# Turns, sines and cosines of the state-space tiles moved from the second attention layer to the first, and a new place for the memory sums behind the bias stores

## The chip, the cores and the metric

The kernel runs on one NeuronCore of a Trainium2 chip. The metric is device microseconds for one execution; a time is the median of several runs.

The core has five instruction streams: TensorE (PE, with its weight loads shown as PEld), VectorE (DVE), ScalarE (ACT), GpSimd (POOL) and SyncE (SP, which here only issues transfers). They run by themselves and are tied together by semaphores: an instruction waits for a count, another raises it. ACT and POOL issue transfers too; such an issue stands in the rows as ACTq or POOL, and the transfer itself runs on 16 DMA engines.

## What is computed

Two transformer blocks over 256 tokens of width 2048, all in fp32. The first has two layers of 16 heads of three kinds, the second has one state-space mixer, one differential attention and a feed-forward part. Cut to what matters here:

```python
for l in range(2):                                   # first block
    h = rms_norm(x, norm_g[l]);  z = h @ w_in[l]     # 6 neighbourhood, 6 dilated, 4 memory heads
    o_na = neighbourhood_attention(..., na_rpb[l])   # needs a bias table for each head
    o_dl = dilated_attention(rope(q), rope(k), v)
    mk, mv = split(rms_norm(mem, mem_norm_g) @ w_mem_kv[l])     # needs the sum of squares of mem
    o_m  = memory_attention(m_q, mk, mv)
    x = x + concat(o_na * silu(..), o_dl * silu(..), o_m * silu(..)) @ w_out[l]
x = rms_norm(x, final_g)

dt   = exp(log_step);  mag = exp(lr * dt)            # second block, state-space mixer
ab_r = mag * cos(li * dt);  ab_i = mag * sin(li * dt)
# s[t] = ab * s[t-1] + B u[t];  y[t] = Re(C s[t]) + d * u[t],  64 groups x 64 states
```

The state-space scan is not run step by step. For each of 32 tiles (two groups of 64 states, 128 partitions) the kernel makes a table from the parameters alone, and stores it to `tab_d` in HBM, where the second block reads it. A table holds the columns e (2 x 128), the lags k (128), the cosines and sines of the angle at 64 chunk starts (64 + 64) and the columns f (2 x 128). Nothing in a table depends on x.

## The kernel before, in words

**Matmuls in two parts.** Each weight chunk (128 x 1024, 512 KB) is loaded by SP into a ring of four `w_raw` buffers, ScalarE makes its high part `w_hi` (`split_hi`, L752), VectorE the rest `w_lo` (`split_lo`, L1404), and TensorE multiplies high by high, high by low and low by high (L2221 to L2223, or L2233 and L2234 where two products are joined). `w_hi` of a chunk may be written once TensorE has used the chunk four before.

**Head periods.** In the first block the unit of work is a head period of eight chunks (four jobs of two). `head_period` is written once for each engine. While the projections of head g stream through TensorE, the attention of head g-1 and the gating of head g-2 run in between: scores (L2258), `softmax_max`, `softmax_exp`, `softmax_scale` on VectorE (reciprocal L1491, two multiplies L1494), the transposition of the probabilities (L2267), and their product with v (L2276). Each layer has 16 head periods, in the order dilated, neighbourhood, memory, with `evac` and `evac_rope` (L1452 to L1461) on VectorE to empty the PSUM banks.

**The memory norm in layer 0.** In the eight periods 4 to 11 ScalarE squares `mem` (`mem_blocks`, L822, L825) and POOL adds the squares up in `msq_sum` (L618, 16 additions of 128 x 256). ScalarE's next square of the loop waits for POOL's addition before.

**Bias tables.** `na_bias` on POOL makes one neighbourhood head's bias of 128 x 512: a transfer into `na_pad_d` (L558), four into `na_raw` (L567), an addition of the mask (L571), and a store to `na_bias_d` (L573), whose landing it waits for before it returns (L574, `na_stored`). POOL makes six of these ahead of the memory sums and six after them.

**The tables in layer 1.** Each of the 16 periods of layer 1 makes two tiles, an even one (between the third and the fourth job's chunks) and an odd one (at the period's end). POOL multiplies up the powers (L597, L598, L601, into `xt`), TensorE transposes e and makes k (L2299, L2301), and then `tile` on ScalarE (L786 to L809) stores f (L789, 128 KB), copies e into `tab_out` (L792), prepares the next tile (L773, L775), computes the sine and cosine of `turns` (Sin table load L800, L801, L803, L805), waits for VectorE's lags and stores e, k, cosines and sines together (L809, 256 KB). VectorE makes `turns` in `tile_turns` (five instructions of 128 x 64, L1520 to L1529) and k in `tile_lags` (four of 32 rows, L1538), the latter not before the store of the tile before has landed (`tab_stored`). Sin and the Tanh of the gate sit in different tables of ScalarE, hence the table loads.

Order on every engine is program order as written; there is no scheduler.

## Time and profile before

| | |
|---|---|
| median of three runs | 2418.33 us (2418.19 to 2419.38) |
| the profiled execution | 2421.73 us |
| its span in the trace | 2420.0 us |
| TensorE busy | 2400.7 us |
| VectorE busy | 1714.1 us |
| ScalarE busy | 1218.7 us |
| GpSimd busy | 526.8 us |
| granted TensorE clock, mean | 0.999 |

The profiled execution took 3.4 us more than the median, and 1.7 us of it lie outside the span. The page gives busy times of the whole; which wait matters is read from the idle time in front of single TensorE instructions, which stands in brackets behind a row with the engine whose work ended it.

### The profile page before, as it was taken

What the parts mean: (1) busy time and instruction counts of PE and PEld (TensorE: products, weight loads), DVE (VectorE), ACT (ScalarE), POOL (GpSimd) and SP (SyncE); (2) the same over time, 40 slices, a digit from 0 to 9 for tenths busy, and PEclk for the clock granted to TensorE, in tenths of its full rate; (3) what the DMA queues carried; (4) which work ended last, traced back from release to release, by engine and by line L of the source; (5) the groups of instructions that cost most, each with busy time, mean ns of one, the idle gap of its engine ahead of it and who ended that gap; (6) DMA issues with size and microseconds to landing.
All of it is one profiled execution on the core that took longest, in us unless ns stands there. A gap on an engine that the chain in (4) does not pass through costs nothing.

```text
span 2420.0 us, 45086 instructions
## 1 busy us (share of the span) xinstructions
PE 2400.7 (99%) x15288; PEld 2170.0 (90%) x15288; DVE 1714.1 (71%) x2644; ACT 1218.7 (50%) x1834; POOL 526.8 (22%) x1002
## 2 busy tenths in 40 slices
PE   9999999999999999999999999999999999999999
PEld 7878888998999999999999999998888888888888
DVE  8877776668888887678888876666555555555556
ACT  6444454455666665556665444444444444444442
POOL 2210032246767773210021221111000000000000
PEclk9999999999999999999999999999999999999999
DMA  7756576666666665565567777756777777777774
GB/s 253 238 177 199 187 227 202 197 195 197 192 205 210 198 197 183 184 203 188 161 196 248 257 224 232 232 193 186 199 191 191 191 191 190 190 190 192 190 190 151
DMA packets 257244, 485.07 MB, mean 200 GB/s; under 512 B 23704, under 2 KB 171876, under 8 KB 256880
## 3 DMA queue, kind: packets, MB, share of 16 engines
q1 hardware_dynamic: 216208, 415.66, 56.5%
q10 hardware_dynamic: 29632, 35.30, 4.6%
q0 software_dynamic: 11296, 32.68, 4.5%
q8 instruction: 67, 1.10, 0.2%
q14 instruction: 41, 0.34, 0.1%
HBM read 455.20 MB, written 31.08 MB: 201 GB/s over the span
## 4 chain that ended last, share of the span: by engine, by line
PE 82%; DVE 7%; DMA 4%; issue 3%; ACT 2%; POOL 1%; ACTq 0%; DVEq 0%; SPq 0%; POOLq 0%
PE z_ps L2233 12%; PE z_ps L2221 9%; PE z_ps L2222 9%; PE z_ps L2223 9%; PE z_ps L2649 7%; PE z_ps L2650 7%; PE z_ps L2655 7%; PE z_ps L2234 6%; DVE w_lo L1404 3%; DMA arena<-na_pad_d 1%; ACT w_hi L752 1%; DMA na_pad_d<-na_one_d 1%; DMA na_bias_d<-arena 1%; PE o_ps L2276 1%; PE s_ps L2258 1%
## 5 line engine op out<-in xcount | busy, mean ns | idle before, releaser
L1404 DVE TENSOR_TENSOR w_lo<-w_raw,w_hi 128x1024 fp32r<-128x1024 f32 x518 | 641.1, 1267 | 215.9 <-ACT w_hi L752 213.9
L752 ACT ACTIVATE w_hi<-w_raw 128x1024 fp32r<-128x1024 f32 x518 | 528.5, 1050 | 229.6 <-PE z_ps L2234 115.7
L2089 DVE TENSOR_TENSOR w_lo<-w_raw,w_hi 128x1024 fp32r<-128x1024 f32 x262 | 320.8, 1226 | 300.5 <-ACT w_hi L1244 300.5
L2233 PE MATMUL z_ps<-x_both,w_hi 128*128 128x512 f32 x1432 | 513.3, 401 | 0.7 <-DVE w_lo L1397 0.5
L1244 ACT ACTIVATE w_hi<-w_raw 128x1024 fp32r<-128x1024 f32 x262 | 277.9, 1061 | 415.3 <-PE z_ps L2655 267.8
L2234 PE MATMUL z_ps<-x_both,w_lo 128*128 128x256 f32 x1432 | 401.2, 280 | 0.0
L2221 PE MATMUL z_ps<-x_both,w_hi 128*128 128x256 f32 x1376 | 397.8, 289 | 1.1 <-DVEq L1941 0.8
L2223 PE MATMUL z_ps<-x_both,w_lo 128*128 128x256 f32 x1376 | 389.3, 283 | 0.0
L2222 PE MATMUL z_ps<-x_both,w_hi 128*128 128x256 f32 x1376 | 389.2, 283 | 0.0
L2233 PEld LDWEIGHTS z_ps<-x_both,w_hi 128*128 128x128 f32 x1432 | 269.6, 188 | 63.6 <-DVE w_lo L1397 0.8
L2649 PE MATMUL z_ps<-w_hi,x_both 128*128 128x512 f32 x704 | 275.0, 391 | 0.0
L2650 PE MATMUL z_ps<-w_hi,x_both 128*128 128x512 f32 x704 | 274.1, 389 | 0.0
L2234 PEld LDWEIGHTS z_ps<-x_both,w_lo 128*128 128x128 f32 x1432 | 270.9, 189 | 0.5
L2221 PEld LDWEIGHTS z_ps<-x_both,w_hi 128*128 128x128 f32 x1376 | 263.7, 192 | 8.1 <-issue 4.8
L2222 PEld LDWEIGHTS z_ps<-x_both,w_hi 128*128 128x128 f32 x1376 | 263.8, 192 | 0.5
L2223 PEld LDWEIGHTS z_ps<-x_both,w_lo 128*128 128x128 f32 x1376 | 263.6, 192 | 0.0
L2221 PE MATMUL z_ps<-y_hi,w_hi 128*128 128x256 f32 x736 | 210.2, 286 | 0.0
L2222 PE MATMUL z_ps<-y_lo,w_hi 128*128 128x256 f32 x736 | 208.2, 283 | 0.0
L2223 PE MATMUL z_ps<-y_hi,w_lo 128*128 128x256 f32 x736 | 208.2, 283 | 0.0
L2655 PE MATMUL z_ps<-w_lo,x_both 128*128 128x512 f32 x704 | 188.2, 389 | 0.0
L2655 PEld LDWEIGHTS z_ps<-w_lo,x_both 128*128 128x128 f32 x704 | 132.1, 188 | 27.5
L2650 PEld LDWEIGHTS z_ps<-w_hi,x_both 128*128 128x128 f32 x704 | 132.2, 188 | 27.2
(474 smaller groups left out, 4186.9 us busy)
## 6 DMA issues: line engine op xcount, KB each, us to landing
w_raw<-in_w SPq DMA_DIRECT2D x624, 512.0 KB, 4.3
w_raw<-in_w SPq DMA_DIRECT2D x160, 256.0 KB, 3.3
w_raw<-in_w SPq DMA_DIRECT2D x80, 384.0 KB, 4.9
w_raw<-in_w SPq DMA_DIRECT2D x80, 128.0 KB, 3.0
tab_d<-arena ACTq DMA_DIRECT2D x32, 256.0 KB, 3.0
res<-tab_d POOLq DMA_DIRECT2D x16, 384.0 KB, 5.6
arena<-tab_d POOLq DMA_DIRECT2D x16, 384.0 KB, 6.1
tab_d<-arena ACTq DMA_DIRECT2D x32, 128.0 KB, 2.8
```

The costliest lines, as they stand in the source:

```text
L752: act.activation(w_hi[:, n % RING, :], w_raw[:, n % RING, :], ACT.Copy).then_inc(w_hi_ready, 1)
L1244: act.activation(w_hi[:, k % RING, :], w_raw[:, k % RING, :], ACT.Copy).then_inc(w_hi_ready, 1)
L1404: dve.tensor_tensor(w_lo[:, n % RING, :], w_raw[:, n % RING, :], w_hi[:, n % RING, :].bitcast(F32), ALU.subtract).then_inc(w_lo_ready, 1)
L2089: dve.tensor_tensor(w_lo[:, k % RING, :], w_raw[:, k % RING, :], w_hi[:, k % RING, :].bitcast(F32), ALU.subtract).then_inc(w_lo_ready, 1)
L2221: pe.matmul(z, wh, hi[:, kt, :], start=(first and i == 0), stop=False)
L2222: pe.matmul(z, wh, lo[:, kt, :], start=False, stop=False)
L2223: m = pe.matmul(z, wl, hi[:, kt, :], start=False, stop=(last and i == len(kts) - 1))
L2233: pe.matmul(z[:], wh, both[:, :, kt, :], start=(first and kt == kts[0]), stop=False)
L2234: m = pe.matmul(z[:, 0, :], wl, both[:, 0, kt, :], start=False, stop=(last and kt == kts[-1]))
L2649: pe.matmul(z[t], x_hi[:, kt, r], hi_w[:, :, i * P:(i + 1) * P], start=(kt == 0), stop=False)
L2650: pe.matmul(z[t], x_lo[:, kt, r], hi_w[:, :, i * P:(i + 1) * P], start=False, stop=False)
L2655: m = pe.matmul(z[t], x_hi[:, kt, t * P:(t + 1) * P], lo_w[:, :, i * P:(i + 1) * P], start=False, stop=(kt == KT - 1))
```

## The change

1. **Turns and trigonometry.** `tile_turns` (VectorE) and the four ScalarE activations of each tile are gone from layer 1. POOL makes the turns of four tiles at once (`four_turns(j)`, eight instructions of 128 x 256), and ScalarE their sines and cosines (`four_trigs(j)`, four activations of 128 x 256 and a store of 256 KB to `tab_d`), once in each of the eight layer-0 periods 4 to 11. The first group's turns stand behind the first two memory sums, the others ahead of theirs. `t_vec` is loaded by SP at the start, not by ScalarE in period 12.
2. **Bias and memory sums on POOL.** The wait for `na_stored` goes from the end of `na_bias` to just before `na_raw` is written again, and is made once more after the twelfth. POOL starts its bias transfers before it waits for the first squares of x.
3. **The stores of a tile.** f is stored as before; e is stored alone from a double buffer (L840 of the new file, 128 KB) right after its copy, with no wait for the lags; the lags have one buffer `k_out` and a store of 64 KB of their own, issued by ScalarE only when it comes to the next tile, ahead of that tile's f. `tile_lags` waits for this store (`k_stored`) where it waited for `tab_stored`.

```diff
@@ na_bias, POOL
                 pool.wait_ge(pad_stored, 16 * lh + 16)
+                reach(pool, na_stored, 16 * lh)
...
                 pool.dma_start(na_bias_d[lh], flat).then_inc(na_stored, 16)
-                pool.wait_ge(na_stored, (lh + 1) * 16)
@@ POOL, layer 0
-            with pool.Fori(0, KT) as n:
-                pool.wait_ge(msq_ready, n + 1)
-                pool.wait_ge(msq_summed, n + 1)
-                pool.tensor_tensor(msq_sum[:], msq_sum[:], msq[:], ALU.add).then_inc(msq_summed, 1)
+            def four_turns(j):
+                reach(pool, trig_ready, j)
+                f, f_hi, f_lo = (ssm_f[:, i, 4 * j:4 * j + 4].unsqueeze(2).to_broadcast([P, 4, NC]) for i in range(3))
+                pool.tensor_tensor(turn_k, times_in, f, ALU.mult)
+                pool.tensor_tensor(turn_d, times_in, f_hi, ALU.mult)
+                pool.tensor_tensor(turns, times_in, f_lo, ALU.mult).then_inc(turn_step, 1)
+                pool.wait_ge(turn_step, 5 * j + 1)
+                pool.tensor_scalar(turn_k, turn_k, ROUND, None, ALU.add).then_inc(turn_step, 1)
...
+                pool.tensor_scalar(turns, turns, 0.5, -0.5, ALU.min, ALU.max).then_inc(turns_ready, 1)
+            for j in range(KT // 2):
+                if j == 0:
+                    sum_mem(2 * j)
+                    sum_mem(2 * j + 1)
+                    four_turns(j)
+                else:
+                    four_turns(j)
+                    sum_mem(2 * j)
+                    sum_mem(2 * j + 1)
             pool.wait_ge(sums_ready, 1)
+            pool.wait_ge(trig_stored, 16 * ST // 4)
@@ tile, ScalarE, layer 1
                 act.wait_ge(ek_done, st + 1)
+                if not (isinstance(st, int) and st == 0):
+                    lags_store(st - 1)
...
-                reach(act, tab_stored, 16 * st)
-                act.activation(tab_out[:, 0:2 * P], tile_bank(bank_of(st, e))[0], ACT.Copy).then_inc(e_ready, 1)
+                reach(act, tab_stored, 16 * (st - 1))
+                act.activation(e_out[e], tile_bank(bank_of(st, e))[0], ACT.Copy).then_inc(e_ready, 1)
...
-                act.wait_ge(turns_ready, st + 1)
-                act.activation(tab_out[:, 3 * P + NC:4 * P], turns, ACT.Sin, scale=TURN)
...
-                act.wait_ge(m_ready, st + 1)
-                act.dma_start(tab_d[st][:, 0:4 * P], tab_out).then_inc(tab_stored, 16)
+                act.wait_ge(e_ready, st + 1)
+                act.dma_start(tab_d[st][:, 0:2 * P], e_out[e]).then_inc(tab_stored, 16)
+            def lags_store(st):
+                act.wait_ge(m_ready, st + 1)
+                act.dma_start(tab_d[st][:, 2 * P:3 * P], k_out).then_inc(k_stored, 16)
+            def four_trigs(j):
+                act.wait_ge(turns_ready, j + 1)
...
+                act.activation(trig_out[:, :, 1, :], turns, ACT.Sin, scale=TURN)
...
+                act.dma_start(tab_d[bass.ds(4 * j, 4), :, 3 * P:4 * P].rearrange("s p x -> p s x"),
+                              sq_sum.rearrange("p a (s x) -> p (a s) x", x=P)).then_inc(trig_stored, 16)
@@ tile_lags, VectorE, layer 1
-                reach(dve, tab_stored, 16 * st)
+                reach(dve, k_stored, 16 * st)
@@ head_period, VectorE (at two places)
-                if l == 1:
-                    tile_turns(2 * h)
@@ head_period, ScalarE, at the end of a memory-norm period
+                if mem is not None:
+                    four_trigs(mem)
```

On POOL, at the end of the first six bias tables, the order was (L573 is the bias store, L618 the memory sum, in a loop, L620 the clearing of `sq_sum` behind the sixteenth):

```order
L573 DMA na_bias_d<-arena 128x512 [waits na_added]
L615 UNCONDITIONAL_BRANCH [waits na_stored]
L615 ISA
L618 TENSOR_TENSOR arena<-arena 128x256 [waits msq_summed,msq_ready]
L615 REGISTER_ALU
L615 COMPARE_AND_BRANCH
L620 MEMSET arena 128x512 [waits sums_ready]
```

and is now (L578 the bias store, L621 the memory sum, L629 to L641 the turns of four tiles):

```order
L578 DMA na_bias_d<-arena 128x512 [waits na_added]
L621 TENSOR_TENSOR arena<-arena 128x256 [waits msq_ready,msq_summed,consts_landed,param_sums]
L621 TENSOR_TENSOR arena<-arena 128x256 [waits msq_summed,msq_ready]
L629 TENSOR_TENSOR arena<-arena,ssm_f 128x256
L630 TENSOR_TENSOR arena<-arena,ssm_f 128x256
L631 TENSOR_TENSOR arena<-arena,ssm_f 128x256
L633 TENSOR_SCALAR arena<-arena 128x256 [waits turn_step]
L635 TENSOR_SCALAR arena<-arena 128x256 [waits turn_step]
L637 TENSOR_TENSOR arena<-arena 128x256 [waits turn_step]
L639 TENSOR_TENSOR arena<-arena 128x256 [waits turn_step]
L641 TENSOR_SCALAR arena<-arena 128x256 [waits turn_step]
L629 TENSOR_TENSOR arena<-arena,ssm_f 128x256 [waits trig_ready]
```

The sums no longer wait for `na_stored`, and eight instructions of turns stand between each pair of sums and the next.

On ScalarE, at an even tile of a neighbourhood period of layer 1, the order was (L830 loads the next head's bias, L789 stores f, L792 copies e, L800 to L805 are the sine and cosine, L809 is the common store):

```order
L830 ISA [waits biased]
L830 DMA arena<-na_bias_d 128x512
L788 ISA
L789 ISA [waits ek_done]
L789 DMA tab_d<-arena 128x2x128
L404 REGISTER_ALU
L792 ACTIVATE arena<-z_ps 128x256 [waits tab_stored]
...
L800 ACT_TABLE_LOAD
L800 ACTIVATE arena<-arena 128x64 [waits turns_ready]
...
L809 REGISTER_ALU [waits m_ready,e_ready,tab_ready]
L809 DMA tab_d<-arena 128x512
```

and is now (L883 the bias, L847 the lags of the tile before, L831 f, L834 the copy of e, L840 its store):

```order
L883 ISA [waits biased]
L883 DMA arena<-na_bias_d 128x512
L828 ISA
L847 ISA [waits m_ready,ek_done]
L847 DMA tab_d<-arena 128x128
L831 ISA
L831 DMA tab_d<-arena 128x2x128
L407 REGISTER_ALU
L834 ACTIVATE arena<-z_ps 128x256 [waits tab_stored]
...
L840 REGISTER_ALU [waits e_ready]
L840 DMA tab_d<-arena 128x256
```

The store of the lags of the tile before stands behind the bias load, ahead of the f store, and the wait for VectorE's lags behind the tile is gone.

On VectorE, between the third job's weights and the scaling of the probabilities, the lags now wait for that store (L1458 is `split_lo`, L1575 the lags, L1545 and L1548 the scaling):

```order
L1458 TENSOR_TENSOR w_lo<-w_raw,w_hi 128x1024 [waits w_hi_ready]
L1571 ISA
L407 REGISTER_ALU [waits e_ready]
L1575 ISA [waits k_stored]
L1575 SCALAR_TENSOR_TENSOR arena<-ident,ssm_em,z_ps 32x128
...
L1575 SCALAR_TENSOR_TENSOR arena<-ident,ssm_em,z_ps 32x32
L1545 RECIPROCAL cols<-cols 128x2 [waits exp_done]
L1548 TENSOR_SCALAR arena<-arena,cols 128x256 [waits factor_ready]
```

The order itself is the one of before; the count that the four lag instructions wait for is raised by another, later store, and the probabilities' scaling stands behind them.

## Rows read from the trace of the kernel before

**Rows 1.** The page: span, and busy time of each engine.

```profile
span 2420.0 us, 45086 instructions
...
PE 2400.7 (99%) x15288; PEld 2170.0 (90%) x15288; DVE 1714.1 (71%) x2644; ACT 1218.7 (50%) x1834; POOL 526.8 (22%) x1002
```

**Rows 2.** Windows: stretch, its length, busy PE, PEld, DVE, ACT, POOL; clock, DMA.

```profile
100.00:200.00 100.00, 94.21 (x530) 81.89 (x528) 82.47 (x166) 47.40 (x74) 15.11 (x20) 0.98 0.62 196
500.00:700.00 200.00, 194.65 (x1357) 180.10 (x1356) 168.25 (x318) 122.47 (x240) 131.58 (x286) 1.00 0.62 196
700.00:950.00 250.00, 250.00 (x1755) 233.54 (x1754) 204.10 (x379) 158.64 (x321) 172.00 (x371) 1.00 0.63 205
```

**Rows 3.** Timeline, PE, layer 0: start, duration, instruction, [idle before <- releaser].

```profile
136.22 1.13 PE L2276 MATMUL o_ps<-arena 128*128 128x256 f32 x4 [2.86 <-ACT arena L857]
...
158.36 1.07 PE L2267 MATMUL p_ps<-ident,arena 128*128 128x128 f32 x4 [2.93 <-DVE arena L1494]
...
159.86 0.63 PE L2233 MATMUL z_ps<-x_both,w_hi 128*128 128x512 f32 x1
...
162.53 0.39 PE L2233 MATMUL z_ps<-x_both,w_hi 128*128 128x512 f32 x1
```

**Rows 4.** Timeline, ACT: two rows of layer 0, and a table load of layer 1.

```profile
133.37 0.42 ACT L825 ACTIVATE arena<-arena 128x256 f32<-128x256 f32 x1 [7.72 <-POOL arena L618]
...
137.47 2.01 ACT L752 ACTIVATE w_hi<-w_raw 128x1024 fp32r<-128x1024 f32 x2
...
775.61 1.28 ACT L800 ACT_TABLE_LOAD   x1
```

**Rows 5.** POOL: two timeline rows, one of the waits, one of the lines.

```profile
20.03 2.57 POOL L545 TENSOR_TENSOR arena<-arena 128x1024 f32<-128x1024 f32 x1 [17.46 <-ACT arena L922]
...
132.61 0.73 POOL L618 TENSOR_TENSOR arena<-arena 128x256 f32<-128x256 f32 x1 [2.08 <-DMA na_bias_d<-arena]
...
POOL na_pad_d L558 <- DMA na_bias_d<-arena: 32.1, 10, 4.4
...
L618 POOL TENSOR_TENSOR arena<-arena 128x256 f32<-128x256 f32 x16 | 14.4, 903 | 162.4 <-ACT arena L825 160.3 <-DMA na_bias_d<-arena 2.1
```

**Rows 6.** Timeline, DVE and POOL: two of layer 0, two beside each other later.

```profile
142.58 2.35 DVE L1404 TENSOR_TENSOR w_lo<-w_raw,w_hi 128x1024 fp32r<-128x1024 f32 x2
...
157.41 0.89 DVE L1494 TENSOR_SCALAR arena<-arena,cols 128x256 f32<-128x256 f32 x2
...
520.39 2.59 POOL L601 TENSOR_TENSOR arena<-arena 128x64 f32<-128x64 f32 x2
...
520.32 2.49 DVE L1404 TENSOR_TENSOR w_lo<-w_raw,w_hi 128x1024 fp32r<-128x1024 f32 x2
```

**Rows 7.** Timeline, an even tile in layer 1: ACT and its queue, DVE, PE.

```profile
772.95 1.06 ACT L752 ACTIVATE w_hi<-w_raw 128x1024 fp32r<-128x1024 f32 x1 [1.26 <-PE z_ps L2223]
773.72 0.39 ACTq L789 DMA_DIRECT2D tab_d<-arena  x1
...
775.18 1.22 DVE L1538 SCALAR_TENSOR_TENSOR arena<-ident,ssm_em,z_ps 32x128 f32<-32x128 f32 x4
...
776.63 0.62 DVE L1494 TENSOR_SCALAR arena<-arena,cols 128x256 f32<-128x256 f32 x2
...
778.41 0.60 PE L2267 MATMUL p_ps<-ident,arena 128*128 128x128 f32 x4
```

**Rows 8.** Timeline, PE, layer 1: three rows with idle time.

```profile
547.23 0.44 PE L2256 MATMUL v_ps<-ident,arena 128*128 128x128 f32 x2 [1.40 <-DVE arena L1436]
...
562.36 0.63 PE L2267 MATMUL p_ps<-ident,arena 128*128 128x128 f32 x4 [1.07 <-DVE arena L1494]
...
591.02 0.41 PE L2299 MATMUL z_ps<-ident,arena 128*128 128x128 f32 x2 [0.80 <-POOL arena L597]
```

**Rows 9.** The f store: landings of L789 from 700 to 950, and one in 773:779.

```profile
DMA to landing us min/median/max: 1.8/2.5/4.6
...
tab_d<-arena ACTq DMA_DIRECT2D x1, 128.0 KB, 4.6
```

92 lines of the change are left out of this document (45 added, 47 removed).

## The prediction

> **What bounds the kernel now.** I read the page first. TensorE is busy 2400.7 of 2420.0 us [rows 1], so the most that any change off TensorE can give back is its idle time and the time it spends at a lower clock. VectorE, ScalarE and GpSimd have room on average, so an instruction less on them counts only where TensorE stands and waits for it. The windows come second, since they say where TensorE's idle time lies: 5.79 us in 100 to 200, 5.35 us in 500 to 700, none in 700 to 950 [rows 2]. The change touches both halves of that: the memory norm lies in the first stretch, the state-space tiles from 520 on. Last, TensorE's timeline gives the waits one by one.
>
> In layer 0 there are two. At 136.22 TensorE waits 2.86 us for ScalarE's L857, at 158.36 it waits 2.93 us for VectorE's L1494 [rows 3]. Both come from one place. ScalarE stood 7.72 us at 133.37 for POOL's memory sum [rows 4], and POOL came to its first sum at 132.61, when its sixth bias store had landed [rows 5]. So everything after ran late: w_hi of the next period at 137.47 [rows 4], w_lo at 142.58, L1494 at 157.41 [rows 6]. Behind the second wait the granted clock fell: the same matmul takes 0.63 us at 159.86 and 0.39 us at 162.53 [rows 3]. That is the lower of the two levels (1.2 and 2.4 GHz) for some 3.4 us; a pair of L2233 and L2234 then takes 0.64 instead of 0.35 us, so about 1.8 us is lost. Together about 7.9 us, counting 0.3 of small idles.
>
> In layer 1 three waits matter: 1.40 us at 547.23 for L1436, 1.07 at 562.36 for L1494, 0.80 at 591.02 [rows 8]. For the last the trace names POOL's L597; VectorE's emptying of the bank by L1454 ended after it, and it is the same bank, so I put it down to VectorE. Several smaller ones make up the 5.35 us.
>
> **The bias tables and the memory sums.** POOL starts its bias chain behind L545, which waited 17.46 us for ScalarE and ran from 20.03 for 2.57 us [rows 5]. The transfers for the bias pad and its copy now go ahead of that wait, which brings the chain forward by about 8 us (my reading of the chain: three transfers, of which two are now done by 20, and 2.57 of L545 beside the third). Each of the five further tables waited for the store before it: 32.1 us in 10 such waits, 3.2 each [rows 5]. That wait now comes behind the pad transfer, which takes longer than the store, so 5 x 3.2 = 16.0 go; the last store's 2.08 us go too. 132.61 - 8 - 16.0 - 2.1 gives 106.5, while ScalarE first needs a sum at 133.37 - 7.72 = 125.65. POOL is 19 us ahead, and the 7.72 us wait goes even if half of this estimate is wrong.
>
> **The turns and the trigonometry in layer 0.** Behind ScalarE's two squares of period 4 there now stand, for the first group, eight POOL instructions of 128 x 256. The nearest row is the memory sum of that shape: 0.73 us alone, 903 ns on average over 16 [rows 5]; so 8 x 0.73 to 8 x 0.90, 5.8 to 7.2 us, plus some 0.1 us for each hop between dependent ones. They start at about 127.4 and end between 133.7 and 136. ScalarE's part is four activations of that shape, 0.42 us for a square [rows 4], 1.7 us, with one gap 2.3 us. The Sin table is in place for the first group; the seven others add one load each, 1.28 us [rows 4], and the Tanh load on the way back. So ScalarE starts w_hi of the next period at 136 to 138, where it started at 137.47 [rows 4]. The change takes 7.7 us out of this place and puts 5 to 8 us back into the same place. TensorE's first wait (2.86 us for L857) goes, since L857 stands ahead of the trigonometry. VectorE's parameter work, which ran from 138.1 to 142.5 between two chunks, now runs while ScalarE waits, and w_lo starts when w_hi has come, 137 to 139 instead of 142.58. L1494 ends 15.7 us after that start (157.41 + 0.89 - 142.58 [rows 6]), so at 153 to 155. TensorE was done with what stands ahead at 158.36 - 2.93 = 155.4, and without the first wait at 152.5. Left of the second wait: 0.7 to 3.6 us; I take 2.1, with 0.4 for a chance of the lower clock. Layer 0 gives back 7.9 - 2.5 = 5.4 us (2 to 7.5). In the other seven periods ScalarE has about 1.7 us in hand at each of eight chunks, where it waits for TensorE, and VectorE 2.0 us ahead of L1494; 3 to 4.3 us of added ScalarE work at the period's end is inside that, and I put it at nothing. If the cover is gone, it costs what exceeds it, at most 1 us in each.
>
> Moving the t_vec load to SP at the start costs nothing: the constants had landed at about 16 us, and their reader, ScalarE, was busy until 18.
>
> **The tables in layer 1.** Gone are 32 x 5 VectorE instructions and, on ScalarE, 32 x 4 activations, the Sin loads (1.28 us each, one to a tile pair or so [rows 4]) and the Tanh loads. VectorE's chain behind the norm of x gets shorter by about 3.9 us, which takes the waits at 547.23 and most of 562.36. With the small ones of the stretch I count 6.5 us gone. Beyond that nothing can be gained: from 700 on TensorE has no idle time to lose [rows 2].
>
> Added is a wait. tile_lags used to wait for the common store of the tile before, long landed. Now it waits for k_stored, which ScalarE issues only when it reaches this tile, just ahead of its f store. At the even tile of a neighbourhood period f was issued at 773.72, lags ran from 775.18, L1494 behind them ended at 776.63 + 0.62 = 777.25, and TensorE's L2267 started at 778.41 without a wait [rows 7]. So the store had 1.46 us until the lags could start and there were 1.16 us of slack behind: it may take 2.6 us from issue to landing at no cost. What stands behind the waiting instruction on VectorE is L1545 and L1548 (the scaling, L1494 before), and TensorE's L2267 waits for them; next the bank of the fourth job.
>
> No row shows a store of 64 KB. The nearest is the f store from the same queue and the same place, with twice the bytes: 1.8, 2.5 and 4.6 us to landing (min, median, max), and 4.6 in the very period above [rows 9]. At the fourteen even tiles from 4 on, it was 2.5 to 2.9 six times, 3.5 once, and 3.8 to 4.6 seven times. The late ones are those where SP's weight load went out shortly ahead of the store; first packets of f then come about 3.3 us after the weight load's issue. Without the Sin loads the two stand at that distance (0.8 to 1.1 us) in nearly every period. I take 3.3 us for k, from 2.3 to 4.1. Cost of an even tile: 3.3 - 2.6 = 0.7 us in ten neighbourhood and memory periods, 7.0 us. In the five dilated ones the bank's emptying (L1454) is already late by 0.80 [rows 8], with no slack for it, so 0.7 + 0.8 = 1.5 us, 7.5 us in all. Odd tiles have room. Layer 1 costs 14.5 - 6.5 = 8.0 us.
>
> Here the Trainium skill speaks against my term. Its page "DMA: Bandwidth & Descriptors", section "Anatomy of one DMA — SWDGE (gpsimd) path", gives about 2.0 us plus bytes over 436 GB/s for one transfer; for 64 KB that is an estimate of 2.15 us, and the new wait would cost next to nothing. The fit is of another queue's path, and the median of 2.5 in [rows 9] agrees with it where the 4.6 does not.
>
> **Sum.** -5.4 + 8.0 = +2.6 us. Against the profiled execution that is 2421.73 + 2.6 = 2424.3; its distance of 3.4 us to the median is kept, so 2418.33 + 2.6 = 2420.9, rounded to 2421.0.
>
> **The rivals.**
>
> *Early k store.* The store lands in 2.5 us or less, as the median of f does. Then the neighbourhood and memory periods cost nothing and the dilated ones 0.7 each, 3.5 us; layer 1 gains 6.5 - 3.5 = 3.0, the whole 8.4: 2409.9. For it: half the bytes of f, ahead of f in the queue. Against it: seven of fourteen even tiles above 3.7 us. This would be the skill's formula come true.
>
> *Late k store.* It lands at about 4.1 us, like the late half of the f stores. It decides from 2.6 us on, one for one. Ten periods at 1.5 and five at 2.3 are 26.5 us, less 6.5 is 20, less 5.4 is +14.6: 2433, slower than before. For it: the 4.6 in the period shown. Against it: that f stood behind a bias load, and the largest is not the usual.
>
> *Late turns.* POOL's turns take longer than 8.6 us because VectorE's work holds them up; ScalarE's w_hi then comes at 139 or later and layer 0 gives nothing. With layer 1 as forecast, +8.0: 2426.3. For it: two small POOL instructions took 2.59 us at 520.39, exactly beside w_lo of 2.49 at 520.32 [rows 6]. Against it: from 127.6 on VectorE has little to do until w_hi comes. The Trainium skill's page "SBUF — State Buffer", section "Who interferes with whom", says that VectorE with two SBUF inputs and GpSimd reading SBUF share a port pair that the first holds for its whole instruction; the pair of rows agrees.
>
> *The sums still late.* If POOL's chain did not get ahead of 125.65, the first wait would stay. It needs 19 us of error; I give it nothing of its own.
>
> **Chances and range.** The forecast case (k at 3.0 to 3.7 us, turns in time) 0.50, its own range 2416 to 2427; early k 0.22; late k 0.18; late turns 0.10. A measurement of this kernel can tell 0.2%, 4.8 us, from no change. Faster than 2413.5: nearly all of early k, 0.20. Slower than 2423.2: late k 0.18, most of late turns 0.07, and 0.17 of the forecast case, together 0.42. Within: 0.38. The range reaches from the early case to the late one: 2410 to 2432.
>
> **What the profile of the changed kernel would show.** ScalarE's 7.72 us wait for the memory sum gone, and one of 5 to 8 us for POOL's L641 at about 128 in its place. TensorE's wait for L857 gone; a wait for L1548 near 152 of about 2 us. In layer 1 idle time of VectorE ahead of L1575, put down to the `tab_d` store, at each even tile, 1.5 to 2 us; TensorE idle ahead of the transposition about 0.7 us each time and busy time below the length of the window between 700 and 950, where it was whole. The lags store's time to landing decides the sign: under 2.6 us I am wrong towards faster, at 4 towards slower. I am also wrong if ScalarE, rid of the trigonometry, gets so far ahead that it issues the store earlier against TensorE than in [rows 7]; its w_hi there waited 1.26 us for TensorE, which speaks against that.

## The result: 25 us slower

| | median | runs |
|---|---|---|
| the kernel before | 2418.86 us (2418.19 to 2420.19) | 4 |
| the changed kernel | 2444.32 us (2441.58 to 2448.68) | 4 |
| ratio | 1.0106, 95% interval 1.0089 to 1.0124 | |

The change costs 25.5 us. The forecast was 2421.0, with a range from 2410 to 2432. The likeliest case had the right sign, not the size, and the time lies outside the range.

The profiled execution of the changed kernel took 2444.82 us, 23.1 more than that of before. Its page, beside [rows 1]:

```profile
span 2443.1 us, 44725 instructions
...
PE 2406.8 (99%) x15288; PEld 2170.6 (89%) x15288; DVE 1684.3 (69%) x2484; ACT 1184.7 (48%) x1718; POOL 593.9 (24%) x1066
```

VectorE and ScalarE do less, GpSimd more, and TensorE stands 36.3 us instead of 19.3. Its own busy time rose by 6.1 us with the same 15288 matmuls, part of it a stretch at the lower clock that the trace of before does not have at that place. The windows of the changed kernel, in the columns of [rows 2]:

```profile
0.00:100.00 100.00, 93.95 (x511) 80.73 (x512) 84.09 (x134) 52.37 (x78) 33.81 (x51) 0.98 0.77 250
100.00:200.00 100.00, 95.08 (x533) 82.37 (x532) 89.96 (x167) 54.60 (x88) 36.85 (x42) 0.98 0.59 187
500.00:700.00 200.00, 190.63 (x1339) 176.49 (x1339) 147.81 (x243) 95.38 (x169) 135.58 (x278) 1.00 0.57 189
700.00:950.00 250.00, 239.23 (x1661) 220.21 (x1661) 169.34 (x268) 116.55 (x216) 173.67 (x372) 1.00 0.56 187
```

From 700 to 950, where TensorE had no idle time before, it now has 10.8 us of it.

**A measure for the rest of this text.** TensorE runs the same 15288 matmuls in the same order in every kernel here. So the start of each one in one trace less its start in another is how late TensorE is at that place, and the difference between two places is what the stretch cost. Against the profiled execution of before, in us, for all kernels of this study (start: to 60 us; layer 0: 60 to 500; layer 1: 500 to 950; times on the clock of the kernel before):

| kernel | start | layer 0 | layer 1 | rest | ratio of times |
|---|---|---|---|---|---|
| changed kernel | +4.5 | -0.8 | +19.0 | +0.4 | 1.0106 |
| e_mask | +3.1 | -0.2 | +23.0 | +0.1 | 1.0101 |
| e_turns | +1.6 | -1.6 | +25.1 | +0.1 | 1.0094 |
| e_start | +0.5 | -0.1 | +21.3 | +1.2 | 1.0091 |
| e_kfirst | +3.7 | +0.4 | +8.6 | +1.1 | 1.0048 |
| e_biaslate | +1.9 | +0.8 | +9.3 | +0.3 | 1.0056 |
| e_kbuf | +1.8 | -0.2 | -4.4 | +0.1 | 0.9992 |
| e_kearly | +3.3 | -0.2 | -5.9 | +1.6 | 0.9986 |
| e_best | -0.7 | +0.4 | -5.9 | +1.3 | 0.9982 |
| e_best2 | +0.1 | +4.6 | -6.0 | +1.4 | 1.0002 |
| e_best3 | -0.5 | -3.2 | -6.3 | +0.7 | 0.9968 |
| b_pool | +1.1 | -6.0 | +0.2 | +0.8 | 0.9969 |
| b_pool2 (the same kernel as b_pool) | -0.6 | -7.8 | -0.1 | 0.0 | 0.9969 |

Each row but the last column comes from one execution. The ratios, here and below, are to the kernel before as it ran beside each experiment: its medians there were 2422.45, 2423.02, 2421.09 and 2422.12 us, some 3 us above the 2418.86 of the first table, so ratios and not medians are to be compared across experiments. The two rows of the same kernel, b_pool and b_pool2, differ by 1.7 us at the start and 1.8 in layer 0; less than 2 us in one cell says nothing.

**Layer 1, +19.0.** One even tile of a neighbourhood period in the changed kernel, to be held against [rows 7]: ScalarE and its queue, then VectorE, then TensorE (L847 is the lags store, L831 f, L840 e).

```profile
701.00 0.37 ACTq L883 DMA_DIRECT2D arena<-na_bias_d  x1
701.69 0.34 ACTq L847 DMA_DIRECT2D tab_d<-arena  x1
702.20 0.39 ACTq L831 DMA_DIRECT2D tab_d<-arena  x1
...
705.23 1.22 DVE L1575 SCALAR_TENSOR_TENSOR arena<-ident,ssm_em,z_ps 32x128 f32<-32x128 f32 x4 [2.05 <-DMA tab_d<-arena]
...
706.68 0.62 DVE L1548 TENSOR_SCALAR arena<-arena,cols 128x256 f32<-128x256 f32 x2
...
707.35 0.65 PE L2297 MATMUL p_ps<-ident,arena 128*128 128x128 f32 x4 [0.88 <-DVE arena L1548]
```

The transfers issued from 701 to 707, with KB and time to landing. The weight load in this view is the one of 703.35, behind the lags store; the one ahead of it, issued at 700.50, took 3.2 us:

```profile
w_raw<-in_w SPq DMA_DIRECT2D x1, 512.0 KB, 4.1
arena<-na_bias_d ACTq DMA_DIRECT2D x1, 256.0 KB, 3.8
tab_d<-arena ACTq DMA_DIRECT2D x2, 128.0 KB, 3.6
tab_d<-arena ACTq DMA_DIRECT2D x1, 64.0 KB, 3.4
```

So the weight load ahead of the store had landed at 703.66, the bias load landed at 701.00 + 3.84 = 704.84, the lags store of 64 KB at 701.69 + 3.40 = 705.09, the lags started at 705.23, and TensorE was late. The waits of VectorE over the whole trace, one row of them, give the count:

```profile
DVE arena L1575 <- DMA tab_d<-arena: 32.7, 15, 3.1
```

Fifteen waits, one in each period of layer 1 after the first, and behind each of them TensorE stood ahead of L2297, 17.1 us in all. (The profile puts 18.8 us of TensorE's waits down to L1548. That number, which the expectations below use, holds 3.4 us of layer 0 and lacks one wait of 1.7 us of layer 1.) In the five dilated periods it then stood 4.1 us more in all ahead of L2329, for the emptying of the bank.

**Layer 0, -0.8.** ScalarE waits for POOL's turns where it had waited for POOL's sum [rows 4], and TensorE's wait for L1548 is no shorter than the one in [rows 3]: 3.39 us. POOL, VectorE, ScalarE, and two of the three idle times of TensorE (the one not shown is 0.48 us at 152.88):

```profile
135.75 1.25 POOL L635 TENSOR_SCALAR arena<-arena 128x256 f32<-128x256 f32 x1
137.08 1.13 POOL L637 TENSOR_TENSOR arena<-arena 128x256 f32<-128x256 f32 x1
...
141.22 3.24 DVE L1391 SCALAR_TENSOR_TENSOR arena<-arena 128x32 f32<-128x32 f32 x8
...
139.83 0.42 ACT L854 ACTIVATE arena<-arena 128x256 f32<-128x256 f32 x1 [6.29 <-POOL arena L641]
...
146.49 0.50 PE L2263 MATMUL z_ps<-x_both,w_hi 128*128 128x512 f32 x1 [1.04 <-DVE w_lo L1458]
...
162.19 0.66 PE L2297 MATMUL p_ps<-ident,arena 128*128 128x128 f32 x4 [3.39 <-DVE arena L1548]
```

**The start, +4.5.** This I had not expected at all. ScalarE and TensorE:

```profile
28.01 1.06 ACT L792 ACTIVATE w_hi<-w_raw 128x1024 fp32r<-128x1024 f32 x1 [3.77 <-DMA w_raw<-in_w]
...
43.36 0.69 PE L2286 MATMUL v_ps<-ident,arena 128*128 128x128 f32 x2 [2.52 <-DVE arena L1490]
...
46.19 0.63 PE L2263 MATMUL z_ps<-x_both,w_hi 128*128 128x512 f32 x1
```

A weight load issued at 20.06 took 7.9 us to land, beside the mask's, issued at 20.10 (7.3 us); VectorE came 2.5 us late to a bank that TensorE needed, and the clock fell to its lower level for 3.4 us behind it (0.63 us for a matmul that takes 0.40).

### The profile page after: what moved, and what is told of

Read it like the earlier page. It is cut to its first block, busy times and chain, and to the rows that moved or that the text cites. A ratio compares the mean times of both kernels' runs of the same rounds, so it can differ in the third digit from the quotient of the medians.

```text
span 2443.1 us, 44725 instructions
## 1 busy us (share of the span) xinstructions
PE 2406.8 (99%) x15288; PEld 2170.6 (89%) x15288; DVE 1684.3 (69%) x2484; ACT 1184.7 (48%) x1718; POOL 593.9 (24%) x1066
## 4 chain that ended last, share of the span: by engine, by line
PE 85%; DVE 6%; DMA 4%; issue 2%; ACT 2%; ACTq 0%; POOL 0%; DVEq 0%; SPq 0%; POOLq 0%
PE z_ps L2263 13%; PE z_ps L2251 10%; PE z_ps L2253 10%; PE z_ps L2252 10%; PE z_ps L2264 7%; PE z_ps L2679 7%; PE z_ps L2680 7%; PE z_ps L2685 7%; DMA tab_d<-arena 2%; DVE w_lo L1458 2%; PE o_ps L2306 1%; PE s_ps L2288 1%; ACT w_hi L792 1%; PE p_ps L2714 1%; PE o_ps L2714 1%
## 5 line engine op out<-in xcount | busy, mean ns | idle before, releaser
L1458 DVE TENSOR_TENSOR w_lo<-w_raw,w_hi 128x1024 fp32r<-128x1024 f32 x518 | 645.9, 1273 | 242.5 <-ACT w_hi L792 240.6
L792 ACT ACTIVATE w_hi<-w_raw 128x1024 fp32r<-128x1024 f32 x518 | 532.3, 1051 | 254.8 <-PE z_ps L2264 132.5
```

The costliest lines, as they stand in the source:

```text
L792: act.activation(w_hi[:, n % RING, :], w_raw[:, n % RING, :], ACT.Copy).then_inc(w_hi_ready, 1)
L1458: dve.tensor_tensor(w_lo[:, n % RING, :], w_raw[:, n % RING, :], w_hi[:, n % RING, :].bitcast(F32), ALU.subtract).then_inc(w_lo_ready, 1)
```

## The experiments

All but b_pool and b_pool2 are the changed kernel with one edit, or several where it says so. Each is named by the label that it has in the table above.

### Why the lags store is late

First, ScalarE's order (e_kfirst): the store ahead of the bias load.

```diff
+                if l == 1 and not norm:
+                    lags_store(2 * h - 1)
                 if prev:
                     load_bias(g, bias_src)
@@ tile
-                if not (isinstance(st, int) and st == 0):
+                if q % 2:
                     lags_store(st - 1)
```

> The changed kernel, with the lags store of an even tile issued by ScalarE just ahead of the bias load instead of just behind it; nothing else. Theory Q (queue): the store is late because it stands behind the 256 KB bias load in ScalarE's own queue; ahead of it it lands in 1.6 to 2.0 us as at the odd tiles (1.56), VectorE's fifteen waits ahead of the lags go, TensorE's fifteen waits for the scaled probabilities (18.8 us) go, and the median falls from 2444 by 19 to 21 us to about 2424. Theory W (weights): it is late because SP's weight load went out about 1 us before; it still takes 3.2 us or more, only its issue is 0.7 us earlier, so 15 x 0.7 = 10 us come back: about 2434.

Measured 2433.70 us (2432.41 to 2435.50), ratio 1.0048 (1.0033 to 1.0063). That is theory W's number (10.4 us came back in layer 1), and theory Q falls: with the bias load no longer ahead of it in ScalarE's queue the store did not get fast (3.5 us in the mean, 3.7 in the changed kernel). Most of what layer 1 got back is the earlier issue, 0.6 us in the mean. The same place in this kernel, ScalarE's queue, SP's, and VectorE:

```profile
754.61 0.34 ACTq L847 DMA_DIRECT2D tab_d<-arena  x1
755.13 0.36 ACTq L883 DMA_DIRECT2D arena<-na_bias_d  x1
...
754.12 3.10 SPq L477 DMA_DIRECT2D w_raw<-in_w  x2
...
757.97 1.22 DVE L1577 SCALAR_TENSOR_TENSOR arena<-ident,ssm_em,z_ps 32x128 f32<-32x128 f32 x4 [1.26 <-DMA tab_d<-arena]
```

and the landings of the transfers issued there:

```profile
w_raw<-in_w SPq DMA_DIRECT2D x1, 512.0 KB, 3.5
arena<-na_bias_d ACTq DMA_DIRECT2D x1, 256.0 KB, 3.3
tab_d<-arena ACTq DMA_DIRECT2D x1, 64.0 KB, 3.2
```

The weight load was issued half a microsecond before, and the small store landed 0.2 us after it. In all fifteen periods the load went out 0.1 to 0.6 us ahead (2.3 in the first), and in all but one the store landed 0.2 to 0.3 us behind it. At the odd tiles of the changed kernel, where the last weight load was issued 5 us and more before, the same store took 1.54 to 1.58 us in thirteen of fifteen cases.

The odd tiles of this kernel show how close the border is. In six of them SP issued a weight load within 0.04 us of the store, and the store took 3.0 to 4.2 us, in four of the six landing 0.2 us behind that load. At the same six tiles of the changed kernel the load went out 0.2 to 0.3 us behind the store, and the store took 1.56 us each time. The border is not sharp: one more store of this kernel, with the load 0.33 us behind it, took 4.0 us. So theory Q's edit also moved the delay to odd tiles: VectorE waits for this store 32.2 us in all here, no less than before (32.7), but there TensorE has room behind it.

Second, the other half (e_biaslate): the store keeps its place in the order, and the bias load goes behind. With the bias load's issue out of its way it goes out 0.4 us sooner after the weight load, so its time is not quite kept.

```diff
-                if prev:
+                if prev and l == 0:
                     load_bias(g, bias_src)
...
                 if l == 1 and not norm:
                     tile(2 * h, 2 * odd, last, ct)
+                if prev and l == 1:
+                    load_bias(g, bias_src)
```

> The changed kernel, with the bias load of layer 1 issued behind the even tile's stores instead of ahead of them; the lags store keeps its time and has the weight load ahead of it alone. Theory W (weights alone): landing stays near 3.7 us and the median near 2444. Theory WB (weights and bias share what the store waits for; the store landed 0.2 us behind the bias load each time in the changed kernel, 0.2 behind the weight load where it went first): it lands 0.2 to 0.5 us behind the weight load, 2.3 to 3.6 us from issue, and about half of the 17 us of TensorE's waits go: 2432 to 2438.

Measured 2435.78 us (2434.03 to 2436.05), ratio 1.0056 (1.0039 to 1.0073): theory WB. The store landed 0.2 to 0.4 us behind the weight load in fourteen of fifteen periods, 3.5 us after its issue in the mean. In the changed kernel it landed 1.1 us in the mean behind the weight load (0.4 to 2.1) and 0.2 to 0.4 behind the bias load. So both count: its landing follows that of what was issued to the DMA engines shortly before, from its own queue or from SP's. It does not follow from its own size, which is the same at the odd tiles. Of the 9.7 us that layer 1 got back, some 4 are the quicker landing (15 x 0.25) and some 6 the sooner issue (15 x 0.4).

Third, is it the wait, or the added traffic (e_kbuf)? Two buffers for the lags, each with a semaphore count of its own, so that no lags wait for the lags store of the tile just before. ScalarE's copy of e now waits for one more store of e than in the changed kernel.

```diff
-        k_out = msq_sum[:, NC:NC + P]
+        k_out = [msq_sum[:, NC:NC + P], ns[:, 0:P]]
@@ tile_lags
-                reach(dve, k_stored, 16 * st)
+                if e:
+                    reach(dve, trig_stored, 4 * ST + 8 * (st - 1))
+                else:
+                    reach(dve, k_stored, 8 * st)
...
@@ tile
-                reach(act, tab_stored, 16 * (st - 1))
+                reach(act, tab_stored, 16 * st)
...
@@ lags_store, with the number of the buffer
-                act.dma_start(tab_d[st][:, 2 * P:3 * P], k_out).then_inc(k_stored, 16)
+                act.dma_start(tab_d[st][:, 2 * P:3 * P], k_out[e]).then_inc(trig_stored if e else k_stored, 16)
```

> The changed kernel, with two buffers for the lags, so that they wait for the store of two tiles before; the order of issues is unchanged. Both theories on the landing expect 3.2 to 4.4 us to landing still at even tiles, with nobody waiting for it. If the wait is what costs (my theory), TensorE's waits ahead of the transposition fall from 18.8 us to under 2 and the median to about 2424. Rival: the cost is contention of the added transfers with the weight loads; then the median stays above 2438.

Measured 2420.36 us (2419.30 to 2421.03), ratio 0.9992 (0.9982 to 1.0001). The lags store still landed late (over all tiles 3.4 us in the median, 2.7 in the changed kernel), with nobody waiting:

```profile
DMA to landing us min/median/max: 1.6/3.4/4.5
```

and TensorE lost nothing from 700 to 950:

```profile
700.00:950.00 250.00, 250.00 (x1760) 233.55 (x1760) 174.51 (x285) 122.29 (x225) 171.52 (x372) 1.00 0.62 196
```

The wait is the cost, the traffic is not. Fourth, one buffer is enough if the store is issued earlier (e_kearly):

```diff
                 if norm and l == 1:
                     tile(0, 0)
+                if l == 1 and not norm:
+                    lags_store(2 * h - 1)
                 if prev:
                     softmax_exp(g - 1, prev and not prev2)
@@ tile
-                if not (isinstance(st, int) and st == 0):
+                if q % 2:
                     lags_store(st - 1)
```

> The changed kernel, one buffer for the lags as it is, but the store of an odd tile's lags issued two chunks earlier, ahead of the softmax of the next period. It has 8 us and more to land, so no lags wait for it, whatever its landing. Median 2421 to 2424, TensorE's waits ahead of the transposition under 2 us in all. If it stays above 2435, the store's own traffic costs, not the wait.

Measured 2419.31 us (2417.29 to 2421.61), ratio 0.9986 (0.9976 to 0.9995). Layer 1 stands at -5.9 here and at +19.0 in the changed kernel: the wait cost 24.9 us, and the moved turns and trigonometry bring 5.9.

### The start

First the mask's transfer (e_mask):

> The changed kernel, with the transfer of the mask issued behind the addition of x's squares again, not ahead of it. Theory M: the mask's transfer at 20.10 beside the weight load at 20.06 made that load land 3 us late (7.93 instead of 4.76 us), and the 4.5 us that TensorE lost between 24 and 46 go: median about 2440, chunk of 20.06 landing within 5 us. Rival: the earlier bias transfers at 3 and 8 us, or t_vec's load, delay the start; then the 4.5 us stay, about 2444.

```diff
-            pool.dma_start(na_mask, ap["na_mask"]).then_inc(pad_filled, 16)
             pool.tensor_tensor(x_sq[0], x_sq[0], x_sq[1], ALU.add).then_inc(xsq_step, 1)
+            pool.dma_start(na_mask, ap["na_mask"]).then_inc(pad_filled, 16)
```

Measured 2446.57 us (2445.64 to 2447.66), ratio 1.0101 (1.0082 to 1.0121). The theory fell in its number: the load of 20 us landed in 5.9 instead of 7.9 us, not within 5, and TensorE still lost 3.1 us to 60. The six kernels with the changed kernel's own start lost 1.6, 1.8, 1.9, 3.3, 3.7 and 4.5 us. So the mask ahead of the addition is not what costs, and one execution varies by some 3 us.

Then all of POOL's first transfers (e_start):

> The changed kernel, with POOL's first bias transfers and the mask behind the addition of x's squares again, as in the kernel before; t_vec is still loaded at the start. Theory: in the runs so far TensorE lost 1.7 to 4.5 us between 24 and 46 whenever the bias transfers were early, with the mask early or not, because POOL's transfers then share the DMA engines with the first weight loads; that loss falls to under 0.5 us. Rival: t_vec's load among the constants causes it, and 1.7 us or more stay. The median itself is dominated by layer 1: about 2441.

```diff
             pool.wait_ge(ones_ident_ready, 4)
+            pool.wait_ge(sq_ready, CH)
+            pool.tensor_tensor(x_sq[0], x_sq[0], x_sq[1], ALU.add).then_inc(xsq_step, 1)
...
-            pool.wait_ge(sq_ready, CH)
             pool.dma_start(na_mask, ap["na_mask"]).then_inc(pad_filled, 16)
-            pool.tensor_tensor(x_sq[0], x_sq[0], x_sq[1], ALU.add).then_inc(xsq_step, 1)
```

Measured 2444.56 us (2442.39 to 2446.14), ratio 1.0091 (1.0074 to 1.0108), and +0.5 us at the start. With the same POOL order the start stood at -0.7, +0.1 and -0.5 in e_best, e_best2 and e_best3, t_vec's load in all of them. That excludes t_vec. POOL's early transfers cost some 3 us of the start in the mean of seven kernels (1.6 to 4.5); the six kernels without them stand between -0.7 and +1.1. Which of the transfers costs, and whether by sharing the DMA engines with the weight loads, no run shows: in e_start the weight load of 20.27 took 6.2 us, longer than in e_mask, and TensorE was late by 0.5 us. Nor was the early start needed: in b_pool, with POOL's start as before, POOL was through with the bias tables at 117.6, and [rows 4] has ScalarE wait from 125.65. The median of e_start itself is not below that of the changed kernel, since layer 1 scatters by as much.

### Layer 0

The first group's turns ahead of the sums (e_turns):

> The changed kernel, with the first four tiles' turns on POOL ahead of the first two memory sums, like the other groups. Theory T: ScalarE's 6.29 us wait for POOL's L641 (which ran from 132.0 to 139.8) is what kept layer 0's gain away: the turns depend on parameters ready at 113.4, run by 121, ScalarE's wait goes, TensorE's waits of 1.04, 0.48 and 3.39 us at 146.5, 152.9 and 162.2 go with the lower clock behind them, 6 to 7 us: about 2438. Rival: VectorE's parameter work and POOL hinder each other anyway and L1548 stays late: 2442 to 2444.

```diff
-                if j == 0:
-                    sum_mem(2 * j)
-                    sum_mem(2 * j + 1)
-                    four_turns(j)
-                else:
-                    four_turns(j)
-                    sum_mem(2 * j)
-                    sum_mem(2 * j + 1)
+                four_turns(j)
+                sum_mem(2 * j)
+                sum_mem(2 * j + 1)
```

Measured 2445.92 us (2441.24 to 2446.86), ratio 1.0094 (1.0071 to 1.0116). ScalarE's 6.29 us wait went, with TensorE's 1.04 and 0.48, as expected. TensorE's wait for the scaled probabilities stayed, and layer 0 gave 1.6 us instead of 6 to 7. In the trace this was the rival's outcome; the median tells nothing here, since layer 1 took 6 us more than in the changed kernel. VectorE's magnitudes (part of the parameter work, `mag` and its powers) and what follows them, and TensorE, in this kernel:

```profile
137.73 2.70 DVE L1386 SCALAR_TENSOR_TENSOR arena<-arena 128x32 f32<-128x32 f32 x8
...
141.12 1.22 DVE L1453 TENSOR_TENSOR w_lo<-w_raw,w_hi 128x1024 fp32r<-128x1024 f32 x1
...
157.56 0.82 PE L2292 MATMUL p_ps<-ident,arena 128*128 128x128 f32 x4 [3.12 <-DVE arena L1543]
```

Then the bias part alone, in the kernel before (b_pool):

```diff
                 pool.wait_ge(pad_stored, 16 * lh + 16)
+                reach(pool, na_stored, 16 * lh)
...
                 pool.dma_start(na_bias_d[lh], flat).then_inc(na_stored, 16)
-                pool.wait_ge(na_stored, (lh + 1) * 16)
...
             for i in range(N_NA):
                 na_bias(N_NA + i)
+            pool.wait_ge(na_stored, DEPTH * N_NA * 16)
```

> The kernel before, with one part of the change alone: POOL waits for a bias store ahead of the next bias load, not behind its own store. No turns in layer 0, the start as before. The bias chain ends some 18 us earlier, so ScalarE's 7.72 us wait at 133.37 and TensorE's 2.86 us wait at 136.22 go. Theory V (VectorE's own parameter work of 4.4 us ahead of w_lo is what is late next): TensorE's second wait, for L1494, stays near 2 us and the gain is 3 to 5 us. Rival: all of the 7.9 us were POOL's, and the gain is 7 to 8 us.

Measured 2416.08 us (2412.76 to 2417.73), ratio 0.9969 (0.9957 to 0.9982): 7 us faster than before. The median is the rival's; the trace has 6.0 us in layer 0. The same VectorE instructions, with no turns on POOL beside them, and TensorE:

```profile
137.25 1.77 DVE L1338 SCALAR_TENSOR_TENSOR arena<-arena 128x32 f32<-128x32 f32 x8
...
139.71 2.35 DVE L1405 TENSOR_TENSOR w_lo<-w_raw,w_hi 128x1024 fp32r<-128x1024 f32 x2
...
155.49 0.66 PE L2268 MATMUL p_ps<-ident,arena 128*128 128x128 f32 x4 [1.54 <-DVE arena L1495]
```

Eight dependent VectorE instructions take 1.77 us alone, 2.70 and 3.24 us beside POOL's turns, and the path runs through them: w_lo of the next period stands behind them in VectorE's order.

They are not the whole of it. In e_best3 below, the last of the study, they run alone again, and TensorE still waits 2.69 us:

```profile
135.96 1.77 DVE L1394 SCALAR_TENSOR_TENSOR arena<-arena 128x32 f32<-128x32 f32 x8
...
141.57 1.28 ACT L895 ACT_TABLE_LOAD   x1
...
154.85 0.66 PE L2300 MATMUL p_ps<-ident,arena 128*128 128x128 f32 x4 [2.69 <-DVE arena L1551]
```

The row between them is a second delay: ScalarE's load of the table for the gate's Tanh. The kernel before has this load once, at 136.18 (b_pool at 132.55, where ScalarE stood waiting for TensorE). In the kernels with the moved sines it comes only with the Tanh itself, right ahead of the w_hi that VectorE's next w_lo waits for, and that w_lo then waits 2.10 us and not 1.43. From the start of that period's first w_lo to the transposition it is 15.8 us in the kernel before, in b_pool and in b_pool2, where no load stands there, and 16.4 us in e_turns, e_best2 and e_best3. In the changed kernel it is 17.0, w_lo being slower beside POOL as well. No run has the turns without this load, so how the rest divides is not shown.

### Can the parts be had together?

Three repairs at once (e_best):

> Three repairs of the changed kernel together: the odd tiles' lags store two chunks earlier, POOL's start as before, the first four tiles' turns ahead of the first sums. By the single runs against the kernel before: start +0.6, layer 0 after it -1.9, layer 1 -5.9, sum -7.2 us, ratio 0.997. Rival: the repairs aren't independent, since what is gained in layer 0 moves the tiles against the weight loads in layer 1; then the sum is above -4 us, ratio 0.9985 or more.

It is the edits of e_kearly, e_start and e_turns in one. Measured 2415.72 us (2414.45 to 2420.41), ratio 0.9982 (0.9973 to 0.9991). It beats the kernel before, by 4 us by the ratio (5 by the medians). The start (-0.7) and layer 1 (-5.9) are as expected; layer 0 (+0.4) is not, and its profiled execution has a stretch at the lower clock of 6.8 us behind the wait at 157, twice the length of before.

Then the sines one period later (e_best2). The edit shown is ScalarE's; POOL's puts the turns, from the second group on, behind the sums.

> As e_best, but ScalarE's sines and cosines one period later (groups 0 to 5 at the ends of periods 5 to 10, group 6 in the middle and group 7 at the end of period 11), and POOL's turns from the second group on behind the memory sums, so that nothing new stands between periods 4 and 5, and no POOL turns run beside VectorE's magnitudes. Theory: layer 0 gave only 1.9 of the 6.0 us that the bias part alone gives because of those two; here it gives 5 to 6, and the sum is -10 to -11 us, ratio 0.9955. Rival: the turns cost wherever they stand, through the ports or ScalarE's table loads; then the ratio is that of e_best.

```diff
+                if mem is not None and not mem_next:
+                    four_trigs(mem - 1)
                 if prev:
                     load_bias(g, bias_src)
...
-                if mem is not None:
+                if mem is not None and not mem_next:
                     four_trigs(mem)
+                elif mem is not None and not (isinstance(mem, int) and mem == 0):
+                    four_trigs(mem - 1)
```

Measured 2421.56 us (2420.17 to 2423.14), ratio 1.0002 (0.9993 to 1.0011). Neither theory had it: the first periods came out better (-3.0 us at 200, the start with it), and then period 11, with two groups in it, and the one behind it lost 7.4 (315 to 345 us). ScalarE at its end:

```profile
317.17 0.42 ACT L852 ACTIVATE arena<-arena 128x256 f32<-128x256 f32 x1 [6.76 <-POOL arena L641]
```

It waited for the second group's turns, which POOL had begun only at 308.80, behind its sums; TensorE then waited 1.45 and 3.94 us, and the clock fell once more.

Last, the eighth group behind period 12 (e_best3), and beside it the bias part alone once more (b_pool2). Of e_best3's edit only what places the eighth group is shown.

> As e_best2, but the eighth group's turns and trigonometry behind period 12, and the seventh at the end of period 11, so that period 11 has one group at its end like the others. Theory: the 7.2 us that e_best2 lost in periods 11 and 12 (1.45 and 3.94 us of waits and a stretch at the lower clock) came from the group placed in the middle of period 11; they go, and the sum against the kernel before is -8 to -9 us, ratio 0.9965. Rival: the eighth group only moves the loss to period 13; then the ratio stays at 0.998 or above.

```diff
+            pool.wait_ge(norm_step, NORM_AT[0] + 12)
+            four_turns(KT // 2 - 1)
             pool.wait_ge(sums_ready, 1)
@@ ScalarE, behind period 12
                     head_period(p0 + m0, l, m0, ap["no_bias"], mem_norm=True)
+                    four_trigs(KT // 2 - 1)
```

> The kernel before with the bias part of the change alone, once more, beside e_best3 on the same chip. It leaves layer 1 as it was. If e_best3 keeps layer 0's gain and adds layer 1's, e_best3 is 2 to 5 us faster than this one; if the moved turns cost in layer 0 what they bring in layer 1, the two are the same. Ratio here 0.997 as before.

Measured on the same chip: e_best3 2414.14 us (2412.48 to 2417.33), ratio 0.9968 (0.9956 to 0.9980), and b_pool2 2414.80 us (2413.17 to 2415.67), ratio 0.9969 (0.9957 to 0.9981). e_best3 is 8 us faster than before and the fastest of the study, by nothing that can be told from b_pool2. Its 500 to 700 window, where [rows 2] had 5.35 us idle:

```profile
500.00:700.00 200.00, 199.31 (x1392) 185.38 (x1392) 155.92 (x260) 99.60 (x181) 148.21 (x301) 1.00 0.62 200
```

The moved turns bring 6.3 us in layer 1 and take back 3 to 5 of them in layer 0 (-3.2 against -6.0 and -7.8), and no place that I tried for them did better. Three changed lines for a wait on POOL reach the same time as the whole change with its repairs.

## Why the prediction was wrong, point by point

Between the two profiled executions the forecast was +2.6 us and the measured difference +23.1. Of the 20.5 us between them, layer 1 has 11.0 (+19.0 for +8.0), layer 0 has 4.6 (-0.8 for -5.4), the start 4.5 (for nothing), and the rest 0.4. The steps that failed are, in this order: the price of the new wait for `k_stored`, the gain of layer 0, and the start, which had no term.

- **What bounds the kernel.** Right: TensorE, and the gain limited to its idle time. e_best3 has TensorE busy 2399.1 of 2410.8 us.
- **The bias chain.** Right. POOL was through at 107.2, where I had 106.5, and the 2.86 us wait went in every kernel with this part. Alone, with POOL's start as before, it is worth 6.0 and 7.8 us of the 7.9 in two traces.
- **The start.** This step failed by omission. I brought POOL's first transfers forward by 8 us and counted only what they release; I put t_vec's load at nothing, which was right, and gave the mask's transfer and those for the bias pad no term at all. They cost about 3 us, 4.5 in the profiled execution.
- **The turns in layer 0.** The step that failed here is "VectorE's parameter work ... now runs while ScalarE waits, and w_lo starts when w_hi has come". It stands behind w_lo and the emptying of a bank, and began at 138.59, as late as before (138.1), beside POOL's turns. Both then hindered each other: turns from 132.0 to 139.8, 7.8 us where I had at most 7.2 and the hops, parameter work 6.6 instead of 4.4 us. w_lo began at 145.23, where I had 137 to 139. A second term failed with it: I took the 15.7 us from w_lo to L1494 as they were, and the Tanh load, which I named but placed nowhere, lies in them (0.66 us). Of the forecast 5.4 us, 0.8 came. The rival *late turns* had 0.10: its outcome came, with the right row [rows 6] and the wrong reason against it, but not its condition, since the turns took 7.8 us and not over 8.6, and TensorE's wait stayed in e_turns, where ScalarE no longer stood for them. In the other seven periods, which I put at nothing, single waits of TensorE up to 1.2 us came (1.13 at 180.89 in e_best3). And a sum was off: L1494 at 153 to 155 against TensorE at 152.5 leaves 0.5 to 2.5 us, not 0.7 to 3.6; the 2.1 that I took lies in both. Here the rule of the Trainium skill that I had cited ("SBUF — State Buffer", section "Who interferes with whom") agrees with the trace in its direction: 1.77 us alone, 3.24 us beside POOL.
- **What layer 1 gains.** Right: 6.5 forecast; -5.9, -5.9, -6.0 and -6.3 in the four kernels where the wait is gone by an earlier store. The three waits of [rows 8] are gone in e_best3 but for 0.08 us, and TensorE's idle time from 500 to 700 fell from 5.35 to 0.69 us.
- **What layer 1 loses.** This is the step that cost most. Its mechanism was right, and it was the first thing named: lags behind the store, scaling behind lags, TensorE behind scaling, at each even tile, 0.8 to 3 us of VectorE's idle time. The term was mis-sized: 14.5 us forecast, 24.9 measured (19.0 + 5.9). The landing was 3.75 us in the mean (3.2 to 4.4), not 3.3; the late rival (4.1) was nearer. And the time free of cost was 2.4 us, not 2.6: 0.14 us passes from landing to lags, 2.12 from lags to TensorE (705.23 to 707.35), and 773.72 to 778.41 [rows 7] is 4.69. (3.75 - 2.43) x 15 is 20 us, and the fifteen waits ahead of the transposition cost 19.1 (the idle 17.1 and the slower matmuls beside it), for which I had 15 x 0.7 = 10.5. The dilated periods' further 0.8 us each was about right: 1.1 in four of them, nothing in the first. The other ten had 0 to 0.3 each that I did not count. For layer 1 as a whole the *late* rival, to which I had given 0.18, came out almost to the microsecond (+20.0, measured +19.0). Half of that is luck: its landing of 4.1 was too long and its 2.6 us of room too much, and the two errors cancel. My reading of the late f stores was also only half right: of the seven, four had a weight load issued 0.4 to 0.7 us ahead of them.
- **The rule on one transfer.** By the Trainium skill's "DMA: Bandwidth & Descriptors", section "Anatomy of one DMA — SWDGE (gpsimd) path", the store would take an estimated 2.15 us. No landing at an even tile of the changed kernel was under 3.17; 1.56 at the odd ones is below the estimate. The measurement decides: here the time went with what was issued ahead of the transfer.
- **The range.** The late case alone gave 2433. It had no part for the start (+3 or more), and assumed layer 0's gain in full. Both misses go the same way, and the range had no case in which the second wait of [rows 3] stays while layer 1 pays.

## What to carry to other kernels

When a wait on one long-landed transfer is replaced by a wait on a fresh one, price it from issue to landing at that place, with everything that is issued to the DMA engines just ahead of it, and not from its size; then either issue it earlier or give it a second buffer. When a change takes work off one stretch, measure each part alone before keeping all of it: here three lines alone gave as much as the best of the whole, and the large move paid in one layer what it won in the other. And an engine that gets ahead starts its transfers earlier: ask what they meet there.

## What the runs showed of the hardware

- A 64 KB store issued 0.1 to 0.6 us behind a 512 KB load of another queue landed 0.2 to 0.3 us after that load, 3.1 to 3.8 us from issue, in thirteen of fourteen cases (e_kfirst). With no 512 KB load issued in the 5 us ahead of it, it landed in 1.56 us (thirteen of fifteen, changed kernel), even where a load went out 0.2 us behind it; with one within 0.04 us of it, it took 3.0 to 4.2 us (six cases, e_kfirst). I had expected two queues to share.
- Small dependent VectorE instructions of 128x32 with both operands in SBUF slow down beside GpSimd's 128x256 ones: eight took 1.77 us alone, 2.70 and 3.24 beside them, while GpSimd's own stayed at 0.73 to 0.90 us. Beside w_lo (128x1024) GpSimd's own went up to 1.60 us, and two of w_lo from 2.35 to 2.88.
- Profiled executions, of one kernel too, differed in where the granted clock fell to the lower level for 3.4 us: at 158 us in that of before, at 9 and 559 us in b_pool, nowhere but in the last 3 us in b_pool2. One such stretch is worth about 1.8 us, by the matmuls of [rows 3], so one trace is no measure of a difference of that size.
